# Rotary stage of a hybrid attention block: key norms from sums per token, three staging steps on another engine, constant matmuls around the last rotation

## What is computed

```python
cbk, cbv = rms_norm(to_heads(cbk), k_gain), to_heads(cbv)
out_b = global_block_attention(apply_axial_rope(rms_norm(to_heads(bq), q_gain), cos, sin),
                               apply_axial_rope(rms_norm(to_heads(bk), k_gain), cos, sin),
                               to_heads(bv), cbk, cbv)
out_a = window_sink_attention(apply_axial_rope(to_heads(aq), cos, sin), apply_axial_rope(to_heads(ak), cos, sin),
                              to_heads(av), cak, cav, sink)
```

## Time and profile before

| | |
|---|---|
| median of three runs | 3442.82 us (3438.43 to 3443.5) |
| the profiled execution | 3442.47 us |
| its span, first to last instruction | 3440.7 us |
| time outside the span | 1.77 us |
| PE busy in the span | 3234.4 us (94%) |
| DVE, POOL, ACT busy | 1777.7, 1382.1, 1009.9 us |
| `norm_and_rotate`, layer 0 | 168.05 to 210.66 us |
| `norm_and_rotate`, layer 1 | 1999.22 to 2037.06 us |

### The profile page before, as it was taken

The page is one execution under the profiler, slowest core; times in us unless marked ns, Lnnn a source line. Parts: engine busy times, 40 slices in busy tenths (PEclk is TensorE's granted clock), DMA queues, the critical chain, the costliest instruction groups (busy, mean ns, idle before and its releaser), DMA issues. The chain is left out here.

```text
span 3440.7 us, 44530 instructions
## 1 busy us (share of the span) xinstructions
PE 3234.4 (94%) x17014; PEld 2739.6 (80%) x17014; DVE 1777.7 (52%) x2884; ACT 1009.9 (29%) x1949; POOL 1382.1 (40%) x1027
## 2 busy tenths in 40 slices
PE   5979989899999999999998979989899999999997
PEld 4768878788788888888886759878787788888886
DVE  8377958685673333333235867936776511311224
ACT  5257742361430000000003347732453300000003
POOL 0154213264444344343444354212354444454454
PEclk9979999999999999999999979999999999999999
DMA  8200023003111212111111610011022111111111
GB/s 332 74 1 1 1 101 107 21 25 123 59 52 62 67 67 68 66 61 61 43 37 66 228 38 1 1 50 50 13 86 80 49 55 49 43 55 49 43 55 50
DMA packets 69808, 214.12 MB, mean 62 GB/s; under 512 B 6816, under 2 KB 19104, under 8 KB 68256
## 3 DMA queue, kind: packets, MB, share of 16 engines
q1 hardware_dynamic: 62224, 183.86, 15.5%
q10 hardware_dynamic: 7440, 28.34, 2.3%
HBM read 192.78 MB, written 19.40 MB: 62 GB/s over the span
## 5 line engine op out<-in xcount | busy, mean ns | idle before, releaser
L205 PE MATMUL ps<-h_hi,f_whi 128*128 128x512 f32 (+1 forms) x1760 | 650.2, 369 | 3.5 <-DVE f_gated L3379 3.5
L206 PE MATMUL ps<-h_lo,f_whi 128*128 128x512 f32 (+1 forms) x1760 | 648.6, 369 | 0.0
L207 PE MATMUL ps<-h_hi,f_wlo 128*128 128x512 f32 (+1 forms) x1760 | 648.0, 368 | 0.0
L3379 DVE TENSOR_TENSOR f_gated<-f_gated,ps 128x512 f32<-128x512 f32 (+1 forms) x110 | 69.6, 634 | 812.6 <-PE ps L207 811.3
L3193 POOL TENSOR_TENSOR f_whi<-f_wraw,small 128x1024 fp32r<-128x1024 f32 x130 | 247.6, 1905 | 555.3 <-PE ps L207 529.7
L3390 DVE SCALAR_TENSOR_TENSOR x_res<-ps,mod,x_res 128x512 f32<-128x512 f32 (+1 forms) x448 | 308.3, 688 | 245.2 <-PE ps L207 244.4
L205 PEld LDWEIGHTS ps<-h_hi,f_whi 128*128 128x128 f32 x1760 | 332.3, 189 | 60.9 <-DVE f_gated L3379 3.9
L206 PEld LDWEIGHTS ps<-h_lo,f_whi 128*128 128x128 f32 x1760 | 332.1, 189 | 55.9 <-issue 1.0
L207 PEld LDWEIGHTS ps<-h_hi,f_wlo 128*128 128x128 f32 x1760 | 332.1, 189 | 55.4
L205 PE MATMUL ps<-f_ahi,f_whi 128*128 128x512 f32 (+1 forms) x896 | 337.4, 377 | 0.6 <-DVE x_res L3390 0.5
L3195 POOL TENSOR_TENSOR f_wlo<-f_wraw,f_whi 128x1024 fp32r<-128x1024 f32 x130 | 327.0, 2516 | 10.2
(11 more groups left out here) (321 smaller groups left out, 6450.7 us busy)
## 6 DMA issues: line engine op xcount, KB each, us to landing
f_wraw<-in_w_ffn SPq DMA_DIRECT2D x130, 512.0 KB, 3.2
ada_w<-in_w_ada SPq DMA_DIRECT2D x80, 512.0 KB, 5.2
later_w<-in_w_ada ACTq DMA_DIRECT2D x32, 512.0 KB, 3.2
o_wraw<-in_w_out SPq DMA_DIRECT2D x28, 512.0 KB, 3.3
wrawc<-in_w_in SPq DMA_DIRECT2D x26, 512.0 KB, 4.2
wrawab<-in_w_in SPq DMA_DIRECT2D x16, 512.0 KB, 6.6
x_res<-x_spill SPq DMA_DIRECT2D x6, 1024.0 KB, 8.1
x_res<-in_xT SPq DMA_DIRECT2D x8, 640.0 KB, 7.4
```

Source lines behind the costliest of these rows:

```text
L205: pe.matmul(out, w_hi, h_hi, start=first, stop=False)
L206: pe.matmul(out, w_hi, h_lo, start=False, stop=False)
L207: return pe.matmul(out, w_lo, h_hi, start=False, stop=last)
L3379: dve.tensor_tensor(g, g, pl.bank(3 + c, tn), ALU.mult).then_inc(u_taken[c], 1)
```

## The change

- The order of the squares is now two chunks of queries (t = 3), the three key chunks, and then the rest. The keys' squares are summed like the queries', in small products per tile of 128 tokens, into bank 6. ScalarE takes one root of 128x20, VectorE one reciprocal of 128x20, ScalarE spreads it to 128x1280 (`k_wide`), and TensorE turns this back with ten products against the identity (`spread`) into banks 7, 0 and 1, from which VectorE multiplies the keys.
- VectorE's list is turn 0, the small reciprocal, turns 1 and 2, three key norms, turn 3, `k_lo`, (in layer 0 two gains,) turns 4 and 5, the query factors, and half of the staging of the first query block. GpSimd keeps the other half. A half has three operations instead of four: the copy is gone.
- ScalarE begins with `bring(0)`. TensorE begins with four rotations.
- `hold_clock` is new: it multiplies constants into bank 7, which nobody reads. Two such 128x512 products stand ahead of `rotate_b(5)` and four behind it, at the end of TensorE's list in the stage.

```diff
+def hold_clock(pl, pe, bank, n):
+
+
+    for _ in range(n):
+        pe.matmul(pl.bank(bank), pl.c(ONES), pl.const[:, 0:512], start=True, stop=True)
...
     q_parts = [(t, c) for t in (3, 4) for c in ORDER if not (last and c == 2)]
-    squares = [(K, c) for c in ORDER] + q_parts
+    keys = [(K, c) for c in ORDER]
+    squares = [(3, 0), (3, 1)] + keys + [part for part in q_parts if part not in ((3, 0), (3, 1))]
+    keys_summed = 2 + len(keys)
     q_tiles = LT if last else TT
     turns_a = [(2, 0), (2, 1), (0, 0), (1, 0), (0, 1), (1, 1)]
     turns_b = [(t, c) for t in range(3, 6) for c in (0, 1)]
-    N, NK = len(squares), len(ORDER)
+    N, NK = len(squares), len(keys)
...
     sq = [pl.at(f"{tag}_sq{s}", [P, 512], F32, kb=169 + 2 * s) for s in range(2)]
-    rt = [pl.at(f"{tag}_rt{s}", [P, 512], F32, kb=173 + 2 * s) for s in range(2)]
-    ri = [pl.at(f"{tag}_ri{s}", [P, 512], F32, kb=177 + 2 * s) for s in range(2)]
+    k_root, k_inv = (pl.at(f"{tag}_k_{x}", [P, TT, 2], F32, kb=173 + 0.25 * n) for n, x in enumerate(("root", "inv")))
+    k_wide = pl.at(f"{tag}_k_wide", [P, TT, 2, HD], F32, kb=174)
...
+    spread_bank = {0: 0, 1: 1, 2: 7}
+    def stage_half(eng, p0):
+
+        h0 = 2 * (p0 // HD)
+        part = lambda z: z[p0:p0 + HD, h0:h0 + 2, :]
+        first = q_src[p0:p0 + HD, :, 0, :]
+        one = pl.small[p0:p0 + HD, 2:3].unsqueeze(2).broadcast_to([HD, 2, P])
+        eng.wait_ge(done[0], 6)
+        eng.tensor_tensor(part(att.q_two), first, one, ALU.mult).then_inc(q_hi_done[h0 // 2], 1)
+        eng.tensor_tensor(part(att.q_pad), first, one, ALU.mult).then_inc(q_padded, 1)
+        eng.wait_ge(q_hi_done[h0 // 2], 1)
+        eng.tensor_tensor(att.q_two[HD - p0:P - p0, h0:h0 + 2, :], first, raw(part(att.q_two)), ALU.subtract) \
+            .then_inc(q_padded, 1)
...
+            bring(0)
             square(0)
             square(1)
-            for n in range(NK):
-                tn = CHUNKS[squares[n][1]][1]
-                act.wait_ge(summed, n + 1)
-                if n >= 2:
-                    act.wait_ge(inverted, n - 1)
-                act.activation(rt[n % 2][:, 0:tn], pl.bank(n % 2, tn), ACT.Sqrt,
-                               bias=pl.small[:, 0:1]).then_inc(rooted, 1)
-                square(n + 2)
-                bring(n)
-            for n in range(NK + 2, N):
+            bring(1)
+            for n in range(2, keys_summed):
                 square(n)
-                if n - 2 < 5:
-                    bring(n - 2)
-            for m in range(N - 2, 5):
-                bring(m)
+            bring(2)
+            act.wait_ge(summed, keys_summed)
+            act.activation(k_root[:, :, :], pl.bank(6)[:, 64:64 + 2 * TT].rearrange("p (t h) -> p t h", h=2),
+                           ACT.Sqrt, bias=pl.small[:, 0:1]).then_inc(k_rooted, 1)
+            square(keys_summed)
+            bring(3)
+            act.wait_ge(k_inverted, 1)
+            act.activation(k_wide[:, :, :, :], k_inv[:, :, :].unsqueeze(3).broadcast_to([P, TT, 2, HD]),
+                           ACT.Copy).then_inc(k_widened, 1)
+            for n in range(keys_summed + 1, N):
+                square(n)
                 act.activation(att.k_hi[other, 0, j, :], pl.qk[own, 0, :], ACT.Copy)
+                if j == 0:
+                    bring(4)
...
+            def sums(n):
 
                 t, c = squares[n]
                 t0, tn = CHUNKS[c]
                 pe.wait_ge(squared, n + 1)
+                    tok = t0 // P + j
+                    if t == K:
+                        out = pl.bank(6)[:, 64 + 2 * tok:66 + 2 * tok]
+                    else:
+                        out = pl.bank(6)[:, tok * HEADS:(tok + 1) * HEADS].rearrange("p (h k) -> p h k", k=2)[:, :, t - 3]
                     mm = pe.matmul(out, sq[n % 2][:, j * P:(j + 1) * P], halves, start=True, stop=True)
                 mm.then_inc(summed, 1)
 
...
-            b = 0
-            for n in range(N):
-                if n < NK:
-                    key_sum(n)
-                else:
-                    query_sums(n)
-                if n < len(turns_a):
-                    rotate_a(n)
-                if n >= 1 and b < 4:
-                    rotate_b(b)
-                    b += 1
-            for m in range(N, len(turns_a)):
-                rotate_a(m)
-            for m in range(b, len(turns_b)):
-                rotate_b(m)
+            def spread(c):
+                t0, tn = CHUNKS[c]
+                for j in range(tn // P):
+                    mm = pe.matmul(pl.bank(spread_bank[c])[:, j * P:(j + 1) * P],
+                                   k_wide[:, t0 // P + j, :, :].rearrange("p h d -> p (h d)"), pl.c(IDENT),
+                                   start=True, stop=True)
+                mm.then_inc(k_spread, 1)
+
+            rotate_a(0)
+            rotate_a(1)
+            rotate_b(0)
+            rotate_b(1)
+            for n in range(keys_summed):
+                sums(n)
+            rotate_a(2)
+            sums(keys_summed)
+            rotate_a(3)
+            rotate_b(2)
+            for n in range(keys_summed + 1, N):
+                sums(n)
+            pe.wait_ge(k_widened, 1)
+            for _, c in keys:
+                spread(c)
+            rotate_a(4)
+            rotate_b(3)
+            rotate_a(5)
+            rotate_b(4)
+            hold_clock(pl, pe, 7, 2)
+            rotate_b(5)
+            hold_clock(pl, pe, 7, 4)
...
-            pool.wait_ge(normed, 2)
-            src = pl.qk[:, 2:4, :].rearrange("p k (t q) -> p k t q", q=P)
-            for n, p0 in enumerate((0, HD)):
-                h0 = 2 * n
-                part = lambda z: z[p0:p0 + HD, h0:h0 + 2, :]
-                if n == 1:
-                    pool.wait_ge(q_padded, 4)
-                pool.wait_ge(done[0], 6)
-                pool.tensor_copy(part(att.qst), src[p0:p0 + HD, :, 0, :]).then_inc(q_copied, 1)
-                pool.wait_ge(q_copied, n + 1)
-                one = pl.small[p0:p0 + HD, 2:3].unsqueeze(2).broadcast_to([HD, 2, P])
-                pool.tensor_tensor(part(att.q_two), part(att.qst), one, ALU.mult).then_inc(q_hi_done, 1)
-                pool.tensor_tensor(part(att.q_pad), part(att.qst), one, ALU.mult).then_inc(q_padded, 1)
-                pool.wait_ge(q_hi_done, n + 1)
-                pool.tensor_tensor(att.q_two[HD - p0:P - p0, h0:h0 + 2, :], part(att.qst),
-                                   raw(part(att.q_two)), ALU.subtract).then_inc(q_padded, 1)
+            stage_half(pool, 0)
...
-                t, c = squares[n]
+                t, c = keys[n]
                 t0, tn = CHUNKS[c]
-                dve.wait_ge(rooted, n + 1)
-                dve.reciprocal(ri[n % 2][:, 0:tn], rt[n % 2][:, 0:tn]).then_inc(inverted, 1)
-                dve.wait_ge(inverted, n + 1)
+                dve.wait_ge(k_spread, n + 1)
                 x = pl.qk[:, qk_slot(t), t0:t0 + tn]
-                dve.scalar_tensor_tensor(out=x, in0=x, scalar=gain_k, in1=ri[n % 2][:, 0:tn],
+                dve.scalar_tensor_tensor(out=x, in0=x, scalar=gain_k, in1=pl.bank(spread_bank[c], tn),
                                          op0=ALU.mult, op1=ALU.mult).then_inc(normed, 1)
...
-            key_norm(0)
-            key_norm(1)
             turn(0)
-            key_norm(2)
-            for m in range(1, 4):
-                turn(m)
+            dve.wait_ge(k_rooted, 1)
+            dve.reciprocal(k_inv[:, :, :], k_root[:, :, :]).then_inc(k_inverted, 1)
+            turn(1)
+            turn(2)
+            for n in range(NK):
+                key_norm(n)
+            turn(3)
+            dve.wait_ge(k_copied, 1)
+            dve.tensor_tensor(att.k_lo[:, 0, :], pl.qk[:, 0, :], raw(k_round[:, :]), ALU.subtract)
...
                                   factor, None, ALU.mult)
-            dve.wait_ge(k_copied, 1)
-            dve.tensor_tensor(att.k_lo[:, 0, :], pl.qk[:, 0, :], raw(k_round[:, :]), ALU.subtract)
+            dve.wait_ge(q_padded, 2)
+            stage_half(dve, HD)
```

More of the change, by code:

```diff
@@ L747, in norm_and_rotate @@
     inv_q = pl.at(f"{tag}_inv_q", [P, TT * HEADS], F32, kb=158.75)
-    squared, summed, rooted, inverted, normed = (pl.sem(f"{tag}_{x}") for x in
-                                                 ("squared", "summed", "rooted", "inverted", "normed"))
+    squared, summed, normed = (pl.sem(f"{tag}_{x}") for x in ("squared", "summed", "normed"))
+    k_rooted, k_inverted, k_widened, k_spread = (pl.sem(f"{tag}_{x}") for x in
+                                                 ("k_rooted", "k_inverted", "k_widened", "k_spread"))
     q_rooted, q_inverted, rot_ready = (pl.sem(f"{tag}_{x}") for x in
@@ L754, in norm_and_rotate @@
     brought = pl.sem(f"{tag}_brought")
-    q_padded, q_copied, q_hi_done, k_copied = (pl.sem(f"{tag}_{x}") for x in
-                                               ("q_padded", "q_copied", "q_hi_done", "k_copied"))
+    q_padded, k_copied = (pl.sem(f"{tag}_{x}") for x in ("q_padded", "k_copied"))
```

(37 more changed lines are left out.)

## The result

The changed kernel takes 3448.97 us (median of 20 runs, 3442.79 to 3452.72) for 3441.68 us before (20 runs, 3438.43 to 3443.5). The recorded ratio, which is not the quotient of the two medians (1.0021), is 1.0019, with a 95% interval of 1.0013 to 1.0025: slower by 0.2%, where 0.2% faster was forecast. Its runs also spread over 10 us, twice as wide as before.

What follows compares the result with a forecast made beforehand. One stage a layer, ended by GpSimd's staging before and by VectorE's list after the change, was taken as the bound; gains of 6.6 (layer 0) and 0.7 (layer 1), 7.3 from 3442.47, gave 3435.2 us, range 3425 to 3445.

Steps and rivals of the forecast that it cites:

- my lengths: Forecast stage lengths: layer 0 at 36.0 us for 42.6, layer 1 at 37.1 for 37.8.
- the clock in the middle of the stage: Key sums, spread and rotations between the stage's start and end: key sums end at 9.6 us, spread takes 2.6.
- gaps that short are survived: TensorE between 11 and 17 us: gaps of 2.4 and 1.4 us keep the clock, stretches of 4.6 do not.
- a fall in the middle: Rival: clock falls at 14 us, back at 24; each layer 4.1 us longer, 3443.4 for both; chance 0.24, one or both.
- The roots: ScalarE: layer 0 `bring(2)` waits until 10.7, copy 0.6, table load 1.28, root done at 12.6; layer 1 at 14.0.
- The norms: VectorE's three key norms, reading PSUM after the spread: 0.70 us each, ending at 22.2 in layer 0.
- `k_lo`'s wait: VectorE after turn 3: `k_lo` waits 2.0 us for ScalarE's rounded copy, then takes 1.6.
- The gains: VectorE in layer 0, ahead of turns 4 and 5: two query gains take 0.45 us.
- The constant products: Around and after `rotate_b(5)`: worth nothing, hidden beside VectorE; TensorE then idles 6.1 us and attention begins without the clock.
- the full clock reaches the first scores: Rival at attention's start: 3.6 us a layer gained, 3428.0 for both layers, 3431.6 for one; chance 0.18.
- The slower rival: Clock stays low, constant products cost 1.71 each, TensorE's list ends the stage: 3455.3, or 3448 with attention warm; chance 0.08.
- the stated 3445: Upper end of the forecast range: both middle falls with the dear norms.

Runs made afterwards that it cites:

- a_mid_products: Changed kernel with seven more constant 128x512 products a layer, spread over the stretch of small products and waits; 3444.34 us, ratio 1.0010.
- a_gains_late: Changed kernel with layer 0's two query gains moved behind turn 5, where GpSimd has stopped; 3445.75 us, ratio 1.0012.
- a_best_attend: a_best with nine instead of four constant products at the stage's end and five in attention, ahead of transposes of heads 0 to 3; 3431.52 us, ratio 0.9970.
- a_best: Changed kernel with wide key sums, late gains, root ahead of `bring(2)`, `k_lo` behind turn 4, three more constant products a layer in TensorE's waits; 3433.97 us.
- after: The changed kernel itself, against the kernel before; 3448.97 us, ratio 1.0019.
- b_split_products: Kernel before with first query block staged half by GpSimd, half by VectorE, and six constant 128x512 products ending TensorE's list; 3438.87 us, ratio 0.9990.

## Why the prediction was wrong

- **Direction: wrong.** The forecast was 3435.2, the result 3449.0. The stages are 15.1 us over my lengths (46.2 and 42.0 for 36.0 and 37.1), 10.2 of them in layer 0; less the 1.1 between the stages, this is the miss of the profiled execution (3449.1), 13.9. Against the median it is 13.8.
- **The failed step** is the clock in the middle of the stage. The sum takes the key sums (end at 9.6) and the spread (2.6) at full clock, on the ground that "gaps that short are survived". I asked only how long TensorE stood idle, and priced a fall in the middle at 4.1 us a layer with a chance of 0.24, with the fall at 14 us. The trace after has the fall at 8.4 us in layer 0, inside the key sums and ahead of the root, in a wait of 0.27 us, and at 10.3 in layer 1; holding the clock made layer 0 5.8 us shorter (a_mid_products). The trace before had hinted at it, in a window that I had read for its clock alone:

```profile
187.60:201.00 13.40, 13.17 (x36) 8.50 (x36) 10.43 (x14) 7.75 (x8) 6.75 (x5) 0.50 0.00 0
```

TensorE is busy in 13.17 of 13.40 us there, 6.0 of it with the query sums, and the clock stays at 0.50 throughout, while the first 4.5 us of the stage had brought it back. Rotations ran in that window too, so it hints and doesn't prove. The change brings ten more such sums a layer, in a place where everything waits.
- **The roots.** The first was to end at 12.6 and ended at 16.3; that of layer 1, forecast at 14.0, started at 13.0. The terms of the forecast (10.7, 0.6, 1.28) give 12.6 for the root's start, so its end was 0.3 too early by its own sum. The chain was right (squares and sums by turns, `bring(2)`, load, root): with `bring(2)` behind the root and the clock held it started at 9.9. Its cost of 1.28 us for the load, on the path as I had it, is measured.
- **The norms.** Ended at 30.6 for 22.2 in layer 0. The operation takes 0.75 (0.70 taken, 0.68 to 0.98 as the ends), the spread 3.84 for 2.6; at full clock it is 2.48.
- **`k_lo`'s wait** for the rounded copy was 1.91 us, forecast 2.0. Right, and 1.80 for the operation (1.6).
- **The gains** were mis-sized: 0.45 forecast from their time beside an idle GpSimd, 2.69 measured. But in a_gains_late only 0.6 us of it was won back by moving them.
- **The constant products:** worth nothing, as forecast, and for the reason given. The gap is 8.3 and 6.6 us, forecast 6.1. The rival that the full clock reaches the first scores did not happen, and its price was too high: 3.6 us a layer forecast, 1.3 to 1.4 measured in a_best_attend.
- **The slower rival** has a time close to the measured one (3448 for 3449.0), but by another way: it has TensorE's list end the stage, with the constant products at half clock. They ran at full clock (3.60 us for the last four) and VectorE ended the stage, so the closeness is chance. The measured time lies above the stated 3445.
- **Reconciliation, layer 0.** a_mid_products at full clock is 4.4 us over my 36.0: 1.65 for the root's end (14.2 for 12.6), behind its two added products; 1.0 more by the norms' end; 2.2 for the gains, of which turns 4 and 5 give 0.6 back; 0.1 more. The other 5.8 us of the 10.2 are the difference to the changed kernel, by the clock. a_best shows stages as short as forecast (35.7 and 34.2) once the clock is held and three steps are moved. Layer 1 was not taken apart in this way.
- What stays open: why the clock fell in layer 0 at 8.4 us and in layer 1 only at 10.3. It also varies from run to run, which is the likely cause of the 10 us spread: of the 20 runs the three shortest, at up to 3443.3, have a mean clock of 0.973, and the six longest, from 3450.7, one of 0.970 to 0.972. That fits, but two runs near the median have 0.973 too, and no trace of a short run is there. The median of a_gains_late wasn't explained either.

## What to carry to other kernels

When a change moves work on TensorE, ask not only how long it will stand idle, but also what kind of product it will run in that time. A stretch of tiny products can look nearly 100% busy and still lose the clock for much that follows. The wide form of the same sum took about the same time here and kept the clock in seven layers of eight, and two or three dense constant products belong where the clock falls in the trace, not at the end of the stage. A product that holds the clock up to a stage boundary pays only if the work behind the boundary keeps it.

## What the runs showed of the hardware

- The granted clock fell from 2.4 to 1.2 GHz between two groups of 32-bit products of 128x2, in a wait of 0.27 us behind 2.29 us of them (after, layer 0, 175.7 us), and stayed at 1.2 GHz with TensorE busy in the next 3.40 of 3.40 us. With 128x128 products for the key sums it stayed at 1.00 through them in seven layers of eight.
- Eight such sums of two columns take TensorE 1.95 us at full clock (after, layer 1), the wide ones 2.05. Two columns save next to nothing. Weight loads are busy in 1.78 of 1.80 us there, so they are the likely bound; that was not tested.
- An idle stretch of 3.0 us ahead of attention ended with the clock at 1.00, which fell 1.2 us later (a_best_attend, layer 0); in one of 2.7 us it fell before the end (b_split_products, layer 0): the length of the idle stretch alone does not settle it.
- VectorE's gain of 128x256 (a tensor-scalar) beside a GpSimd operation: 2.69 us for two, 0.60 beside an idle one.
